# Another order for the masks and the split results of sliding attention, on VectorE and ScalarE

## The reference, cut to what matters

```python
def swa_sink_mixer(q, k, v, sinks):            # 6 query heads, 2 key heads, width 64, chunks of 128
    q = rope(q.reshape(b, s, 6, 64), 16, ROPE_THETA); k = rope(k.reshape(b, s, 2, 64), 16, ROPE_THETA)
    ...
    sc = einsum('bcqhgd,bckhd->bchgqk', qb, kb) * 64 ** -0.5   # a chunk against itself and the one before it
    sc = where(0 <= qpos - kpos < 128, sc, NEG_INF)
    probs = softmax(concatenate([sc, sink], -1), -1)[..., :-1]
    o = einsum('bchgqk,bckhd->bcqhgd', probs, vb)
```

## Time and profile before

| | |
|---|---|
| median of 3 runs | 1238.25 us (1237.32 to 1238.42) |
| profiled execution, its own time | 1237.87 us |
| its span, first to last instruction | 1236.1 us |
| PE busy | 1221.3 us, 99% of the span |
| DVE busy | 841.5 us, 68% |
| ACT busy | 616.1 us, 50% |
| POOL busy | 136.6 us, 11% |
| granted TensorE clock, mean | 0.996 of full speed |

### The profile page before, as it was taken

How to read it: one execution, slowest core, us unless ns; L and a number is a source line. 1 busy time by engine, 2 the same in 40 slices (tenths; PEclk the granted TensorE clock), 3 DMA queues, 4 the chain that set the end, 5 groups by cost and what they waited for, 6 DMA issues and landing times.

```text
span 1236.1 us, 20397 instructions
## 1 busy us (share of the span) xinstructions
PE 1221.3 (99%) x7873; PEld 1113.4 (90%) x7873; DVE 841.5 (68%) x1365; ACT 616.1 (50%) x1204; POOL 136.6 (11%) x208
## 2 busy tenths in 40 slices
PE   9999999999999999999999899999999999999998
PEld 8988888999999998888899789889999999888887
DVE  5675544988888853268976746468888887433788
ACT  7444334555555642237664444264655555322474
POOL 2003531000000000003030036210000000000120
PEclk9999999999999999999999999999999999999999
DMA  7322232233333353320242222322333333444001
GB/s 247 107 66 88 68 103 68 69 97 109 103 103 103 103 188 142 131 68 18 86 124 65 90 65 69 103 70 68 112 110 105 103 103 120 154 153 170 18 17 69
DMA packets 124464, 122.31 MB, mean 99 GB/s; under 512 B 5200, under 2 KB 108752, under 8 KB 124368
## 3 DMA queue, kind: packets, MB, share of 16 engines
q1 hardware_dynamic: 123680, 120.48, 31.0%
q10 hardware_dynamic: 688, 0.53, 0.2%
HBM read 118.90 MB, written 2.10 MB: 98 GB/s over the span
## 4 chain that ended last, share of the span: by engine, by line
PE 91%; DVE 6%; ACT 2%; issue 1%; POOL 0%; DVEq 0%; ACTq 0%
PE bank L993 28%; PE bank L995 28%; PE bank L994 28%; PE bank L1203 2%; DVE w_lo L1882 2%; ACT prob L1671 1%; PE bank L1322 1%; DVE rope_a L1909 1%; PE bank L1262 1%; PE bank L1306 1%; DVE rope_b L1910 1%; DVE prob L2247 0%; PE bank L1283 0%; DVE tiny L2249 0%; PE bank L1298 0%
## 5 line engine op out<-in xcount | busy, mean ns | idle before, releaser
L993 PE MATMUL bank<-w_hi,h_hi 128*128 128x384 f32 (+2 forms) x564 | 201.7, 358 | 0.6 <-DVE w_lo L1882 0.5
L994 PE MATMUL bank<-w_lo,h_hi 128*128 128x384 f32 (+2 forms) x564 | 195.7, 347 | 0.0
L1880 DVE TENSOR_TENSOR w_lo<-raw,w_hi 128x1024 fp32r<-128x1024 f32 x70 | 83.7, 1233 | 133.7 <-ACT w_hi L1400 133.4
L993 PE MATMUL bank<-h_hi,w_hi 128*128 128x256 f32 x568 | 161.0, 284 | 0.1
L995 PE MATMUL bank<-h_hi,w_lo 128*128 128x256 f32 x568 | 160.7, 283 | 0.0
L994 PE MATMUL bank<-h_lo,w_hi 128*128 128x256 f32 x568 | 160.7, 283 | 0.0
L995 PE MATMUL bank<-w_hi,h_lo 128*128 128x384 f32 (+2 forms) x468 | 158.4, 339 | 0.0
L1400 ACT ACTIVATE w_hi<-raw 128x1024 fp32r<-128x1024 f32 x70 | 70.6, 1053 | 160.6 <-PE bank L995 160.6
L995 PE MATMUL bank<-w_hi,mid_lo 128*128 128x512 f32 x352 | 137.0, 389 | 0.0
L993 PE MATMUL bank<-T_hi,w_hi 128*128 128x256 f32 x448 | 126.8, 283 | 0.0
L994 PE MATMUL bank<-T_lo,w_hi 128*128 128x256 f32 x448 | 126.8, 283 | 0.0
(11 more groups left out here) (294 smaller groups left out, 2912.0 us busy)
## 6 DMA issues: line engine op xcount, KB each, us to landing
raw<-in_w_ffn_in SPq DMA_DIRECT2D x88, 512.0 KB, 3.9
raw<-in_w_ffn_out SPq DMA_DIRECT2D x44, 512.0 KB, 4.1
raw<-in_w_in SPq DMA_DIRECT2D x40, 384.0 KB, 4.0
raw<-in_w_out SPq DMA_DIRECT2D x16, 512.0 KB, 3.9
gw<-in_w_gate SPq DMA_DIRECT2D x16, 512.0 KB, 3.3
raw<-in_w_in SPq DMA_DIRECT2D x10, 512.0 KB, 4.3
raw<-in_w_ple SPq DMA_DIRECT2D x4, 512.0 KB, 6.3
x<-in_x_in SPq DMA_DIRECT2D x3, 512.0 KB, 7.4
```

Source lines behind the costliest of these rows:

```text
L993: pe.matmul(out_ap, a_hi, b_hi, start=start, stop=False, skip_group_check=True)
L994: pe.matmul(out_ap, a_hi, b_lo, start=False, stop=False, skip_group_check=True)
L1880: last = dve.tensor_tensor(lo, raw[q % RAWS][:, cols], hi, ALU.subtract)
```

## The change

What VectorE and ScalarE did under the events `swa_PT` and `swa_o` gets events of its own: `swa_mask` (VectorE's two masks), `swa_yhi` (ScalarE's high part of the result) and `swa_ylo` (VectorE's low part). PE's order stays as it is, and so does every instruction. Three things move:

- `swa_mask` of tile 2 goes from step 28 to step 26: on VectorE ahead of the rotation of bq's block at step 27 and of the low parts of a's first strip, and still behind the rotation at step 26. PE's transposes that it waits for stay at step 28. The masks of the other tiles stay where they were.
- `swa_yhi` of tiles 0 and 1 goes on ScalarE ahead of the exponentials of the next tile (steps 19 and 24). In the case of tile 0 it also passes the high parts of bv's first strip.
- `swa_ylo` of tile 0 goes on VectorE ahead of `swa_norm` of tile 1 and of the low parts of bv's first strip. That of tile 1 was ahead of `swa_norm` of tile 2 already.

Tiles 2 and 3 keep the places of their results. The number of instructions, DMAs and buffers is the same.

```diff
--- before.py
+++ after.py
@@ -119,8 +119,19 @@
     for c in range(TILES):
         put(10 + c, "swa_T", c)
         u = (13, 18, 23, 28)[c]
-        for step, name in zip((0, 1, (2, 1, 2, 2)[c], 5, 7), ("swa_cur", "swa_prev", "swa_norm", "swa_PT", "swa_o")):
-            put(u + step, name, c)
+        put(u, "swa_cur", c)
+        if c:
+            put(u + (1 if c < 3 else 2), "swa_yhi", c - 1)
+        put(u + 1, "swa_prev", c)
+        if c:
+            put(u + (1 if c < 2 else 2), "swa_ylo", c - 1)
+        put(u + (2, 1, 2, 2)[c], "swa_norm", c)
+        put(u + 5, "swa_PT", c)
+        put(u + (5, 5, 3, 5)[c], "swa_mask", c)
+        put(u + 7, "swa_o", c)
+        if c == TILES - 1:
+            put(u + 7, "swa_yhi", c)
+            put(u + 7, "swa_ylo", c)
         u = (33, 37, 41, 45)[c]
         for step, name in zip((0, 2, 3), ("ret_T", "ret_sc", "ret_o")):
             put(u + step, name, c)
@@ -1679,9 +1690,9 @@
                     act.wait_ge(pt_masked0, layer * TILES + c + 1)
                     act.activation(ptu[c % 2][:, 0:3, :], swa_bank(c, 0)[:, 0:BW].rearrange("p (h t) -> p h t", h=3),
                                    ACT.Copy).then_inc(pt_copied0, 1)
-                elif kind == "swa_o":
-                    c = e[1]
-                    y_split(layer, e, swa_bank(c, 1)[:, 0:BW].rearrange("p (k t) -> p k t", k=3),
+                elif kind == "swa_yhi":
+                    c = e[1]
+                    y_split(layer, ("swa_o", c), swa_bank(c, 1)[:, 0:BW].rearrange("p (k t) -> p k t", k=3),
                             y_hi[:, 5:8, c * P:(c + 1) * P])
                 elif kind == "ret_T":
                     c = e[1]
@@ -2258,7 +2269,7 @@
                     step(dve.reciprocal(rl[o], rl[o]))
                     done(dve.tensor_tensor(prob[o][:], prob[o][:], rl[o][:, :, None].to_broadcast([P, 6, P]),
                                            ALU.mult), swa_pn)
-                elif kind == "swa_PT":
+                elif kind == "swa_mask":
                     c = e[1]
                     dve.wait_ge(swa_PT, layer * TILES + c + 1)
                     for g in range(2):
@@ -2267,9 +2278,9 @@
                         b3 = swa_bank(c, g)[:, 0:BW].rearrange("p (h t) -> p h t", h=3)
                         done(dve.tensor_tensor(ptl[c % 2][:, 3 * g:3 * g + 3, :], b3, mask3(T_("lowT")), ALU.mult),
                              (pt_masked0, swa_PTm)[g])
-                elif kind == "swa_o":
-                    c = e[1]
-                    y_split(layer, e, swa_bank(c, 1)[:, 0:BW].rearrange("p (k t) -> p k t", k=3),
+                elif kind == "swa_ylo":
+                    c = e[1]
+                    y_split(layer, ("swa_o", c), swa_bank(c, 1)[:, 0:BW].rearrange("p (k t) -> p k t", k=3),
                             y_hi[:, 5:8, c * P:(c + 1) * P], y_lo[:, 5:8, c * P:(c + 1) * P])
                 elif kind == "ret_sc":
                     c = e[1]
```

## The result

The changed kernel takes 1225.48 us (median of four runs, 1224.77 to 1225.55) against 1237.96 us (four runs, 1237.32 to 1238.42). The ratio is 0.9898, with a 95% interval of 0.9881 to 0.9915: 12.5 us less. The forecast was 1225.7 us.

The account below looks back on a forecast made before the run. PE, busy 99% of 1236.1 us, bounds the kernel, so only its idle time and slow clock can be won. 5.25 + 6.25 + 0.53 + 0.5 = 12.5 us off 1238.25 gives 1225.7 us, range 1223.8 to 1231.

Parts of the forecast that it names:

- The wait at `swa_prev` of tile 3: PE's 3.6 us wait a layer for ScalarE's score copies goes, with the slow clock behind it: 5.25 + 6.25 us.
- The chain as told: What made `swa_prev` of tile 3 late: VectorE's rotation and low parts, first mask, `ptu` copy, score copies, PE.
- Waiting against clock: Split of the loss at tile 3: 3.6 us idle in each layer, clock 1.6 and 2.7 us.
- The waits for `y_lo`: PE's wait for `y_lo` at the score matmul line goes in both layers: 0.53 + 0.5 us gained.
- The small steps: Times from tile 2's masks through `ptu` copy and score copies to PE's `swa_prev` of tile 3, 0.95 us to spare.
- VectorE's new wait: VectorE's wait for PE's transposes ahead of tile 2's masks: about nil, at most 0.3 us.
- The low parts: VectorE's work put behind tile 2's masks: from 89.7 to 92.35, asked for by PE only at step 36.
- Tile 3's scaling: The next thing to be late on VectorE: done at 99.7, PE asks at 101.5, 1.8 us to spare.
- `y_lo` of tile 1 no longer waits: On VectorE, lets tile 2's scaling end before PE asks at 85.98; otherwise PE would wait 0.3 us a layer.
- The first rival: A wait of 1 to 2 us a layer stays at `swa_prev`, clock loss still gone: 1228 to 1231 us, chance 0.12.
- The rival at tile 3: Scaling late for PE's transposes gives the gain back: 1231 to 1236 us, chance 0.05; slower than before, 0.03.

Follow-up runs that it names:

- masks_only: The changed kernel with the split results back in their old places, so only tile 2's masks move: 1226.66 us, ratio 0.9910.
- mask_between: The changed kernel with tile 2's masks behind the rotation of step 27, still ahead of the low parts: 1225.85 us, ratio 0.9904.
- mask_late8: The changed kernel with eight scratch VectorE operations after the wait for the transposes and ahead of tile 2's masks: 1235.56 us, ratio 0.9985.
- pe_filled: The kernel before, with 20 unread matmuls a layer on PE ahead of its wait at `swa_prev` of tile 3: 1233.76 us, ratio 0.9969.
- mask_late4: The changed kernel with four scratch VectorE operations after the wait for the transposes and ahead of tile 2's masks: 1227.96 us, ratio 0.9919.
- norm_late7: The changed kernel with seven scratch VectorE operations ahead of tile 3's scaling, after its wait for the exponentials: 1231.25 us, ratio 0.9944.
- yhi1_back: The changed kernel with tile 1's `y_hi` behind tile 2's exponentials again: 1225.43 us, ratio 0.9900.
- results_only: The changed kernel with tile 2's masks back behind the low parts, so only the split results move: 1234.12 us, ratio 0.9972.

## Why the prediction was right

**The wait at `swa_prev` of tile 3.** Summed as 5.25 + 6.25 = 11.5 us of waiting and clock; `masks_only` measured 10.9, which its interval (9.0 to 13.2) doesn't tell from 11.5, and the pattern in the changed kernel is back to 6.91 us. The chain as told (low parts, first mask, `ptu` copy, score copies, PE) is shown from both sides: by `mask_between`, where only the low parts are passed and 0.23 us stay, and by `mask_late8`, where only the masks are late and 3.53 us come back.

**Waiting against clock.** The prediction split it into 7.2 and 4.3 us. `pe_filled` puts the clock at 3.8 by the medians and at 4.15 by the two profiles, so the term holds within what can be told. It was read from one execution, and the length of the slow stretch differs from layer to layer (1.6 and 2.7 us lost) and from run to run; that the whole forecast came within 0.2 us is in part luck, as the medians of the kernel before alone lie half a us apart.

**The waits for `y_lo`.** Summed 1.0 us; the changed kernel is 1.2 us below `masks_only` (1.6 if each is taken against the kernel before beside it), which the spread can't tell from 1.0.

**The small steps.** Masks at 87.05 forecast, 86.91 measured; score copies done at 88.95 and 88.76; PE's request at 89.9 and 89.96; to spare 0.95 and 1.2 (and again 1.2 by `mask_late4`). VectorE's new wait: at most 0.3, measured 0.24. The low parts: from 89.7 forecast, from 89.50 measured. Tile 3's scaling done at 99.7 forecast and 99.41 measured, PE's request at 101.5 and 101.59; 1.8 to spare forecast, 2.2 by `norm_late7`.

**Where a step was off.** The prediction called it needed that `y_lo` of tile 1 no longer waits, at a price of 0.3 us a layer otherwise. `yhi1_back` shows no price. The term held VectorE's times of tile 2 fixed while it moved PE's by 0.53; in truth the exponentials of tile 2 start at 81.13 and not 81.46, because ScalarE's score copies and so bv's low parts moved as well. The first rival was mis-sized: it let waits of up to 2.5 us go without clock loss, from waits of 0.4. That holds at 1.16 us (`mask_late4`) and no longer at 1.87 (`norm_late7`, layer 1) and 2.87 (`results_only`): with 2.9 us a layer the kernel takes 1234.1 us, where the rival's way of counting gives 1231.5. The rival at tile 3 gave no price to the clock up to 3 us of waiting and said only that it could be more. Neither case came about, so the forecast didn't hang on it.

## What to carry to other kernels

When the busiest engine waits, follow the wait back to the engine whose queue held something that was ready to be done, and ask what stood ahead of it there and when that work is needed: here 2.7 us of low parts that PE asks for 22 us after they are written stood ahead of a 0.5 us mask. Price such a wait by the distance between starts before and behind it, against the same pattern where it isn't disturbed, so that what the clock takes afterwards is in the sum. And size what is to spare at the new place by putting known work in front: it showed that the first us beyond 1.2 counts in full, and that at 3.5 us of waiting some 3 us of clock in the two layers come on top.

## What the runs showed of the hardware that was not expected

TensorE's clock fell behind waits shorter than the 3.6 us that the kernel before shows, and at 1.9 us not each time. Behind 1.16 us (`mask_late4`) it stayed at 1.00. In `norm_late7` it stayed at 1.00 behind the 1.86 us of layer 0 and was at 0.54 for 3.6 us behind the 1.87 of layer 1, about 1 us after PE had begun to work again; one of its four runs has a clock of 0.999 and 1229.15 us, the other three 0.998 and about 1231.4. In the profile of `results_only` waits of 2.87 and 2.88 us brought it down in both layers. In one the 12 matmuls behind the wait were already slow (1.65 us), in the other it fell only after those 12 (0.94 us):

```profile
93.29 1.65 PE L1273 MATMUL bank<-cT 64*128 64x128 f32 x12 [2.87 <-ACT prob L1674]
...
705.19 0.94 PE L1273 MATMUL bank<-cT 64*128 64x128 f32 x12 [2.88 <-ACT prob L1674]
```

The Trainium skill, page "TensorE: Matmul & The Clock Gate", section "Part 1: The HAM clock gate", says that the gate looks at windows that run freely and do not start with the kernel. The trace agrees in so far as a wait of one length now brings the clock down and now doesn't; no run here shows the windows themselves.

Nor does the length of the wait set the loss. Taken from the distance of the blocks of steps 29 and 31, less the 6.91 us of the undisturbed pattern and less the wait, the slow clock took 2.7 and 1.6 us in the two layers of `results_only` (waits of 2.9), 1.6 and 1.6 in `mask_late8` (3.5), 1.6 and 2.7 in the kernel before (3.6), and, by the distances given at `norm_late7`, nothing and 1.6 there (1.9). In the two stretches that lost 2.7 the clock was at 0.50 from `swa_prev` to the end of the block; in the others a part of that work ran at full speed. So a wait has no one price: by these profiles the clock adds nothing at 1.2 us, nothing or 1.6 us at 1.9, and 1.6 or 2.7 us from 2.9 on.
